# An expert gate on ScalarE: one sigmoid for an exponential, an addition and a reciprocal

## The reference

```python
def moe_ffn(h, w_router, router_bias, wg, wu, wd):
    scores = jax.nn.sigmoid((t @ w_router).astype(jnp.float32))
    ...            # best group of four experts, the two best in it, gates normalised
    hg = jnp.einsum('nd,edf->nef', t, wg)
    hu = jnp.einsum('nd,edf->nef', t, wu)
    act = jax.nn.silu(hg) * hu * combine[:, :, None].astype(t.dtype)
    out = jnp.einsum('nef,efd->nd', act, wd)
```

## Time and profile before

| | |
|---|---|
| median of 3 timed runs | 2150.41 us (2144.57 to 2153.1) |
| the profiled execution | 2144.65 us, its span 2143.0 us |
| busy share of the span: TensorE, VectorE, ScalarE | 89%, 77%, 67% |
| moved by DMA | 575.14 MB, mean 268 GB/s |
| mean granted TensorE clock | 0.953 |

### The profile page before, as it was taken

The page is one execution under the profiler, slowest core; times in us unless marked ns, Lnnn a source line. Parts: engine busy times, 40 slices in busy tenths (PEclk is TensorE's granted clock), DMA queues, the critical chain, the costliest instruction groups (busy, mean ns, idle before and its releaser), DMA issues.

```text
span 2143.0 us, 31258 instructions
## 1 busy us (share of the span) xinstructions
PE 1913.6 (89%) x8974; PEld 1482.3 (69%) x8974; DVE 1645.5 (77%) x2365; ACT 1433.7 (67%) x2272; POOL 99.1 (5%) x86
## 2 busy tenths in 40 slices
PE   7999998986999999999489999989779999999993
PEld 6877776774767767667377787767657677677672
DVE  5567666557999999999465667765569999999993
ACT  5555565443888888888355565653348988888882
POOL 0000000001010010000000000000010000100000
PEclk9999999987999999999789999999869999999996
DMA  6434443545999999999444444435469999999993
GB/s 256 158 138 157 148 156 112 184 191 213 388 391 389 406 392 406 384 399 403 187 153 143 139 156 159 142 114 196 184 219 391 394 393 407 391 393 395 390 381 138
DMA packets 83005, 575.14 MB, mean 268 GB/s; under 512 B 11760, under 2 KB 12016, under 8 KB 13264
## 3 DMA queue, kind: packets, MB, share of 16 engines
q1 hardware_dynamic: 75600, 542.01, 65.7%
q0 software_dynamic: 7296, 31.85, 4.5%
HBM read 567.52 MB, written 23.07 MB: 276 GB/s over the span
## 4 chain that ended last, share of the span: by engine, by line
PE 48%; DVE 20%; issue 17%; ACT 8%; DMA 6%; DVEq 1%; ACTq 0%; POOLq 0%; POOL 0%; SPq 0%
PE bank L775 9%; DVE wl L1091 9%; PE bank L777 9%; PE bank L776 9%; ACT wh L522 5%; PE bank L940 4%; PE bank L942 3%; PE bank L941 3%; PE bank L924 3%; DVE wT L1520 3%; PE bank L926 2%; DMA raw<-in_expert_units 2%; DVE xh L1511 1%; DMA proj<-picks 1%; PE bank L907 1%
## 5 line engine op out<-in xcount | busy, mean ns | idle before, releaser
L1091 DVE TENSOR_TENSOR wl<-raw,wh 128x1024 fp32r<-128x1024 f32 x640 | 764.8, 1221 | 315.8 <-ACT wh L522 314.9
L522 ACT ACTIVATE wh<-raw 128x1024 fp32r<-128x1024 f32 x640 | 664.4, 1054 | 423.9 <-PE bank L777 342.5
L1091 DVE TENSOR_TENSOR wl<-proj,wh 128x1024 fp32r<-128x1024 f32 x384 | 451.9, 1220 | 33.6 <-ACT wh L522 33.1
L924 PE MATMUL bank<-wh,xh 128*128 128x512 f32 x1024 | 435.6, 425 | 44.7 <-DVE wl L1091 41.4
L522 ACT ACTIVATE wh<-proj 128x1024 fp32r<-128x1024 f32 x384 | 395.0, 1053 | 77.4 <-PE bank L942 55.9
L775 PE MATMUL bank<-wh,xh 128*128 128x512 f32 x1024 | 419.8, 410 | 5.9 <-DVE xl L1128 3.1
L926 PE MATMUL bank<-wl,xh 128*128 128x512 f32 x1024 | 407.6, 398 | 0.0
L777 PE MATMUL bank<-wh,xl 128*128 128x512 f32 x1024 | 405.3, 396 | 0.0
L776 PE MATMUL bank<-wl,xh 128*128 128x512 f32 x1024 | 404.5, 395 | 0.0
L924 PEld LDWEIGHTS bank<-wh,xh 128*128 128x128 f32 x1024 | 195.3, 191 | 148.3 <-DVE wl L1091 109.3
L775 PEld LDWEIGHTS bank<-wh,xh 128*128 128x128 f32 x1024 | 196.2, 192 | 49.5 <-DVE wl L1091 9.9
(11 more groups left out here) (208 smaller groups left out, 1593.0 us busy)
## 6 DMA issues: line engine op xcount, KB each, us to landing
raw<-in_expert_units SPq DMA_DIRECT2D x192, 1024.0 KB, 11.0
proj<-in_expert_units SPq DMA_DIRECT2D x192, 1024.0 KB, 11.3
raw<-in_in_units SPq DMA_DIRECT2D x96, 1024.0 KB, 4.8
raw<-in_out_units SPq DMA_DIRECT2D x32, 1024.0 KB, 4.8
proj<-picks POOLq DMA_DIRECT2D x8, 1024.0 KB, 8.1
expert_rows<-rows POOLq DMA_DIRECT2D x4, 1024.0 KB, 4.3
x<-in_x SPq DMA_DIRECT2D x2, 1024.0 KB, 6.7
wide<-in_norms POOLq DMA_DIRECT2D x2, 1024.0 KB, 5.1
```

What stands on the lines that cost most here:

```text
L522: act_(wh[:, h % CUT, :], ring[j][:, h % 2 * HALF:(h % 2 + 1) * HALF], ACT.Copy)\
L924: mm(bank[m][:, :], stacked[b][:, 2 * h + c, :], wh[:, j, k], start=(h + c == 0), stop=False)
L1091: v.tensor_tensor(wl[:, h % CUT, :], ring[(first + h // 2) % slots][:, h % 2 * HALF:(h % 2 + 1) * HALF], wh[:, h % CUT, :].bitcast(F32), A ...
```

## The change

The exponential becomes ScalarE's sigmoid of z itself. The addition and the reciprocal on VectorE are gone, `gate_silu` waits for the sigmoid instead of VectorE's own last step, and stands at GATE_OUT + 4 for every expert. The semaphore has a new name.

```diff
-                def gate_exp():
+                def gate_sigmoid():
                     e.wait_ge(S["gate_turned"], t_.due("gate_turned"))
-                    act_(gate_act, bank[6][:, 0:4 * SLOTS], ACT.Exp, scale=-1.0).then_inc(S["sig_exp"], 1)
+                    act_(gate_act, bank[6][:, 0:4 * SLOTS], ACT.Sigmoid).then_inc(S["sigmoid"], 1)
...
                         if h == GATE_OUT[first] + 2:
-                            gate_exp()
+                            gate_sigmoid()
...
-                def gate_plus():
-                    e.wait_ge(S["sig_exp"], t_.due("sig_exp"))
-                    v.tensor_scalar(gate_act, gate_act, 1.0, None, ALU.add).then_inc(S["dve_done"], 1)
-
-                def gate_inverse():
-                    e.wait_ge(S["dve_done"], t_.due("dve_done"))
-                    v.reciprocal(gate_act, gate_act).then_inc(S["dve_done"], 1)
-
                 def gate_silu():
-                    e.wait_ge(S["dve_done"], t_.due("dve_done"))
+                    e.wait_ge(S["sigmoid"], t_.due("sigmoid"))
                     v.tensor_tensor(gate_act, bank[6][:, 0:4 * SLOTS], gate_act, ALU.mult).then_inc(S["dve_done"], 1)
...
-                        if h == GATE_OUT[first] + 3:
-                            gate_plus()
                         if h == GATE_OUT[first] + 4:
-                            gate_inverse()
-                        if h == GATE_OUT[first] + (4 if first else 5):
                             gate_silu()
```

More of the change, by code:

```diff
@@ L385, in trunk @@
             "start_landed const_landed x_landed out_stored router_ready hi_ready lo_ready cut_free block_out "
-            "xt_banked xt_hi xt_lo gate_out gate_turned up_out up_turned sig_exp act_ready act_hi act_lo "
+            "xt_banked xt_hi xt_lo gate_out gate_turned up_out up_turned sigmoid act_ready act_hi act_lo "
             "out_ready out_free proj_free "
@@ L1085, in _ @@
             t_ = tally(e, start={"cut_free": CUT, "block_out": 2}, tells=False,
-                       counted=("hi_ready", "xt_hi", "sig_exp", "act_hi", "up_turned", "dve_done"))
+                       counted=("hi_ready", "xt_hi", "sigmoid", "act_hi", "up_turned", "dve_done"))
             def cut(h, slots=RAW, first=0):
```

## The result

The kernel with the sigmoid took 2130.59 us (median of 4 runs, 2122.7 to 2131.43), the kernel before, with one more run beside it, 2149.27 us: ratio 0.9905, 95% interval 0.9882 to 0.9927. That is 18.7 us faster, where the forecast said 6.8. The stated range, 2112 to 2158, held; the forecast's own, 2140 to 2148, did not. A second session with the same kernel gave 2127.68 us, ratio 0.9898 (0.9878 to 0.9919). The profiled execution is the fastest of the four, 2122.7 us with a span of 2121.0.

What follows compares the result with a forecast made beforehand. Expert stages were taken as bound by VectorE and weight transfers within 1%, the transfers absorbing the steady saving. Stage ends gave -7.6 us, tables +0.8: -6.8 us, 2143.6 off the median; range 2112 to 2158.

Steps and rivals of the forecast that it cites:

- a deeper queue that moves more: Rival, expert stages: an always deep load queue lifts the mean rate 1 to 2%, 10 to 20 us more gain; chance 0.17.
- the signs of being right: Expert stages: VectorE busy 60 us less, ScalarE waiting tens of us for weights, landings 17 to 20 us, mean 394 to 400 GB/s.
- The steady part: Expert stages between their ends: VectorE's saving becomes ScalarE's wait for weight transfers, so charged at nothing.
- The transfers' limit: Expert stages: DMA engines taken as at their limit, 394 GB/s shown, while the full saving would need about 420.
- The saving on VectorE: Gate of each expert: add and reciprocal removed, 1.86 us an expert, 59.5 us over 32.
- That VectorE alone stands against the transfers: Expert stages: by the waits VectorE, 96% busy, is the bound, its demand within 1% of the transfers' supply.
- The 3.2 us in hand at the end of a stage: End of each expert stage: last loads land before they are wanted, giving back 3.2 us a layer.
- The sigmoid's duration: ScalarE's gate step: sigmoid taken at 0.37 us like the exponential, no effect on the time.
- The tables: ScalarE's activation table loads: five or so more at most, none per expert, charged 0.4 us a layer.
- The first, room in the transfers: Rival, expert stages: transfers had room, so every expert saves its 1.86 us, time 2091; chance 0.12.
- The second and third: Rivals, load queue: deeper moves more, 2124 to 2134, chance 0.17; or deeper moves less, 2168, chance 0.10.
- The fourth: Rival, ScalarE: tables reloaded in each expert, 22 us slower if all on the path, 2172; chance 0.03.

Runs made afterwards that it cites:

- the light one: Kernel after with one of three matmuls of each down block (low part of the weights) left out, all bytes loaded: 2103.45 us, ratio 0.9813.
- TensorE light: One of three matmuls of each down block left out: kernel before 2112.91 us, kernel after 2103.45, kernel after with half the experts' bytes 2052.76.
- The pads: Kernel after with a VectorE reciprocal on dead data put back in each expert's turn: at half 3 2171.44 us, at half 20 2137.09.
- the early kernels: TensorE's turns of the next expert's rows moved to halves 0 and 5: before 2152.02 us, after 2130.26, after with half the bytes 2105.37.

## Why the prediction was right or wrong

**The range and the sign held; the reason did not.** The measured 2130.59 lies in the part of the range that was kept for a deeper queue that moves more (2124 to 2134), and the queue got shallower: that the range held is luck. Of the signs of being right only the mean of the stretch came, 399 in 526 to 1018; no wait for a transfer came, and no median landing of a stretch read in layer 1 was over 13.7 us. The step that failed is "I charge the steady part of the stage at nothing: the same bytes over engines that are busy already end at the same moment". The steady part gave most of the gain. From the second gate product of layer 1 to the last the kernel before takes 460.86 us (558.89 to 1019.75) and the kernel after 452.57 (559.03 to 1011.60), 8.3 less in 14 intervals. 14 x 0.42 = 5.9 of that are the shorter experts. The other 2.5 are two experts of the kernel before that waited for transfers and the like of which the kernel after has none (in one profile of the kernel before and two of the kernel after):

```profile
886.91 0.41 DVE L1524 TENSOR_TENSOR wT<-bank,wT 128x256 f32<-128x256 f32 x1
920.97 0.41 DVE L1524 TENSOR_TENSOR wT<-bank,wT 128x256 f32<-128x256 f32 x1
954.99 0.41 DVE L1524 TENSOR_TENSOR wT<-bank,wT 128x256 f32<-128x256 f32 x1
```

These are 34.06 and 34.02 us against 32.81 (products of the gate, as above). Layer 2 has one such, 33.91 us. Together: 2 x 5.9 + 2.5 + 1.1 = 15.4 us of the 18.7.

Most of the rest lies in the first turn and at the end of each stage. The first gate product stands at the same half in both kernels. From it to TensorE's last matmul of the stage the kernel before takes 514.87 us in layer 1 (529.51 to 1044.38) and 513.21 in layer 2 (1597.49 to 2110.70), the kernel after 504.80 (532.64 to 1037.44) and 504.83 (1583.97 to 2088.80): 10.1 and 8.4 less, 18.5 in all. That leaves about 1.8 and 1.5 us a layer beside the 14 intervals. The first turn has gate and up halves alone, where VectorE's need is the larger, so nearly the whole 1.86 us would count once; no run tries this. In front of that product the two profiles differ by the granted clock too (497 to 560: 0.89 before, 0.82 after; 1553 to 1616: 0.74 and 0.91), and their spans by 22.0 us where the medians differ by 18.7.

**The transfers' limit was put too low.** I took the 394 GB/s of the kernel before for the limit; but for its few waits it was its demand. The kernel after moved 403 to 404 without a wait, and those kernels that do wait for transfers show 397 to 405 (as the light one above). The reading that "the engines work off a backlog without ever emptying it" came from the share, and the share of 1.00 at 388 GB/s shows that it cannot carry this. Landing times did not carry it either: they fell when the demand rose. Why they fell was not tried; the loads are issued at other moments now. Nor is the limit one number: the kernel before waited while it moved 395 GB/s, and the first three experts of the light kernel moved 409 without a wait. In the kernel after too the landings grow within layer 1, from a median of 7.2 us (659 to 692) to 13.7 (921 to 953), so it ends the stage before its reserve is gone and has little to spare.

**The saving on VectorE** was right (1.86 by the rows, 1.80 with TensorE light). **That VectorE alone stands against the transfers** was wrong: TensorE was left out of the list. Each down half has six matmuls at 0.233 us, 1.40 us, against 1.15 for a cut; in the gate and up halves it is four, 0.93 against 1.15. TensorE's timeline of the kernel after, the first and the last of a run of rows between which none shows idle time, from the eighth half of one turn to the second turning of rows (half 17):

```profile
673.69 0.50 PE L924 MATMUL bank<-wh,xh 128*128 128x512 f32 x1 [0.33 <-DVE wl L1091]
...
688.50 0.40 PE L942 MATMUL bank<-wh,actT 128*128 128x512 f32 x1
688.83 0.71 PE L907 MATMUL bank<-const,proj 64*128 64x64 f32 x8
```

VectorE, up to four halves ahead, had its reciprocal in this part. TensorE's busy time had stood in the very rows read, 469.27 of 492 us, nearly as high as VectorE's 472.29. The removed work sat in the part in which TensorE needs almost as long. The pads show it, 1.31 us at half 3 and 0.21 at half 20, and so does the light TensorE, with which the same removal is worth 1.80. That VectorE alone sets the other part is not shown: of TensorE's idle time in 560 to 1000 12.6 us end with a cut of VectorE and 10.8 with ScalarE's copy of the up sums, and no run takes that copy away.

**The 3.2 us in hand at the end of a stage** were no term of their own: the reserve is only given back by a consumer that runs dry, and this one never does. The same load of the kernel after is issued at 2051.3, lands 9.4 us later and is cut at 2066.59, so 5.9 us are in hand now. **The sigmoid's duration** was right, 0.368 us. **The tables**: 31 loads against 25, where I expected up to five more, and no cost seen against the 0.8 us in the sum.

**The rivals.** The first, room in the transfers, was right in its premise and wrong in its price: 59.5 us need VectorE to be the only bound. The second and third, that depth changes what is moved, had no occasion, since the queue got shallower (a median landing of 9.2 us over the run for the loads into `raw`, 11.0 before); the light and the early kernels, with landings near 18 us, moved 397 to 405, which speaks for neither strongly. The fourth did not happen. What the Trainium skill, DMA: Bandwidth & Descriptors, says in "Where 436 GB/s comes from", a ceiling of 435 GB/s, was not reached as a mean in any run: those limited by transfers stand at 397 to 405, dips around gathers included.

## What to carry to other kernels

An engine's need has to be added up for each part of a repeating turn, not for the whole turn: an instruction costs what the engine is late by in the part where it stands, here 1.31 us or 0.21 us for the same 1.75 us reciprocal. When two engines show the same busy share, removing work from one gains only until the other is reached; both belong in the sum. A DMA share of 1 says that transfers are always outstanding, not that they are at their limit: see whether the consumer waits for them, or halve the bytes.

## What the runs showed of the hardware

The DMA engines' share was 1.00 to 1.01 at 388, 395 and 403 GB/s. Landing times of 1024 KB loads fell from a median of 9.1 to 7.7 us (593 to 626) while the rate stayed (398 and 399); over 560 to 1000 the rate rose from 395 to 403. In the light kernel, with gaps in TensorE's work, the granted clock's mean in 526 to 1000 was 0.98 where it is 1.00 in the same stretch of the kernel after and of those with the pads.
